# mLSTM stage: gate sums by store and broadcast load, queries and keys turned by 32x32 blocks and transfers

## What is computed

```python
proj = x @ w_in                                   # q, k, v, o, gates
k = k * 128 ** -0.5
log_i = gates[:4];  log_f = log_sigmoid(gates[4:])
# for each chunk of 128 tokens, each head, with the state (C, n, m):
b = cumsum(log_f)
d = b[:, None] - b[None, :] + log_i[None, :]      # causal, else -inf
m_t = max(b + m, max(d, -1))
w = exp(d - m_t)
qk = (q @ k.T) * w
num = qk @ v + s_inter * (q @ C)
den = sum(qk, -1) + s_inter * (q @ n)
h = num / max(abs(den), exp(-m_t))
# the state C, n from keys scaled by exp(g - m_new), and the values
```

## Time and profile before

| | |
|---|---|
| median of 3 runs | 1367.62 us (1362.96 to 1368.35) |
| the profiled execution | 1362.45 us, span 1360.7 us |
| TensorE busy | 1342.6 us, 99% of the span |
| GpSimd busy | 1144.6 us, 84% |
| VectorE busy | 653.0 us, 48% |
| ScalarE busy | 651.9 us, 48% |
| DMA queue q1 (SP) | 249.91 MB, 58.2% of 16 engines |
| mean granted clock of TensorE | 0.998 |

### The profile page before, as it was taken

One profiled execution on the slowest core, in us unless ns is written; L12 is line 12 of the kernel. 1 busy time (PEld: TensorE's weight loads), 2 busy tenths in 40 slices (PEclk: granted clock), 3 DMA queues, 4 the chain that ended last, 5 costly groups with the idle time before them and its releaser, 6 DMA issues.

```text
span 1360.7 us, 19512 instructions
## 1 busy us (share of the span) xinstructions
PE 1342.6 (99%) x6659; PEld 1115.8 (82%) x6659; DVE 653.0 (48%) x1584; ACT 651.9 (48%) x745; POOL 1144.6 (84%) x913
## 2 busy tenths in 40 slices
PE   8999999999999999999999999999999999989997
PEld 6888888888888888888888778888888887778886
DVE  6233344654333356523333885333346447874224
ACT  6444454546444456444444676444446344434431
POOL 6999977849999969999998539999978989789982
PEclk9999999999999999999999999999999999999999
DMA  8666654536665555766558426666545799997640
GB/s 275 216 209 204 204 186 141 186 107 225 196 192 193 197 171 168 240 210 214 185 185 217 139 70 205 209 196 194 193 155 179 221 268 270 256 247 230 206 164 32
DMA packets 230608, 263.75 MB, mean 194 GB/s; under 512 B 75884, under 2 KB 166804, under 8 KB 230548
## 3 DMA queue, kind: packets, MB, share of 16 engines
q1 hardware_dynamic: 201876, 249.91, 58.2%
q10 hardware_dynamic: 28672, 13.05, 3.7%
HBM read 253.49 MB, written 9.44 MB: 193 GB/s over the span
## 4 chain that ended last, share of the span: by engine, by line
PE 90%; DVE 5%; DMA 2%; ACT 1%; issue 1%; ACTq 1%; SPq 0%; DVEq 0%
PE tb L2203 9%; PE gu L2203 9%; PE acc L2113 7%; PE acc L2114 7%; PE acc L2116 7%; PE acc L2150 6%; PE acc L2153 6%; PE acc L2158 6%; PE gu L2113 5%; PE gu L2114 5%; PE tb L2209 4%; PE gu L2209 4%; PE gu L2116 3%; PE gu L2121 2%; DMA hidden_T<-h_bounce 1%; PE tb L2116 1%
## 5 line engine op out<-in xcount | busy, mean ns | idle before, releaser
L664 POOL TENSOR_TENSOR w_lo<-w_raw,w_hi 128x512 fp32r<-128x512 f32 x896 | 1139.6, 1317 | 189.0 <-ACT w_hi L697 186.6
L697 ACT CAST w_hi<-w_raw 128x2048 fp32r<-128x2048 f32 x225 | 428.0, 1910 | 185.9 <-DMA w_raw<-in_w_in 46.6
L2203 PE MATMUL gu<-xT,w_hi 128*128 128x512 f32 x512 | 202.4, 395 | 0.0
L2203 PE MATMUL tb<-xT,w_hi 128*128 128x512 f32 x512 | 202.2, 395 | 0.0
L2113 PE MATMUL acc<-w_hi,xT 128*128 128x512 f32 x496 | 197.9, 399 | 0.0
L2114 PE MATMUL acc<-w_lo,xT 128*128 128x512 f32 x496 | 193.8, 391 | 0.0
L2116 PE MATMUL acc<-w_hi,xT 128*128 128x512 f32 x468 | 183.1, 391 | 0.0
L1419 DVE TENSOR_TENSOR arena<-gu,arena 128x256 f32<-128x256 f32 x64 | 27.2, 425 | 300.6 <-PE gu L2203 300.6
L2209 PE MATMUL tb<-xT,w_lo 128*128 128x256 f32 x512 | 140.3, 279 | 0.0
L2209 PE MATMUL gu<-xT,w_lo 128*128 128x256 f32 x512 | 139.8, 279 | 0.0
L2113 PE MATMUL gu<-w_hi,xT 128*128 128x512 f32 x312 | 123.4, 395 | 1.1 <-ACT xT L742 1.1
(11 more groups left out here) (364 smaller groups left out, 1974.4 us busy)
## 6 DMA issues: line engine op xcount, KB each, us to landing
w_raw<-in_w_ffn_in SPq DMA_DIRECT2D x176, 512.0 KB, 4.7
w_raw<-in_w_ffn_out SPq DMA_DIRECT2D x88, 512.0 KB, 4.2
w_raw<-in_w_in SPq DMA_DIRECT2D x80, 512.0 KB, 4.8
w_raw<-in_mlstm_w_in SPq DMA_DIRECT2D x24, 512.0 KB, 4.3
w_raw<-in_w_ple_gate SPq DMA_DIRECT2D x16, 512.0 KB, 4.3
w_raw<-in_w_kv SPq DMA_DIRECT2D x16, 512.0 KB, 4.3
w_raw<-in_mlstm_w_out SPq DMA_DIRECT2D x8, 512.0 KB, 4.4
w_raw<-in_diff_w_q SPq DMA_DIRECT2D x8, 512.0 KB, 5.0
```

The lines of the kernel that those rows point to most:

```text
L664: ins = pool.tensor_tensor(w_lo[:, slot.spl, cols], w_raw[:, slot.raw, cols], w_hi[:, slot.spl, cols].bitcast(F32), ALU.subtract)
L697: nc.scalar.copy(w_hi[:, slot.spl, :], w_raw[:, slot.raw, :]).then_inc(hi_ready, 1)
L2203: return mm(pair_of(j), w_hi[:, slot.spl, at:at + P], xT[:, 4 * half + k, :, :].rearrange("p a c -> p (a c)"), start=(half == 0 and k == 0 ...
```

## The change

It has two parts.

*Gate sums.* `diag` and `spread` are gone. VectorE's a (128 x 8 values) is stored by SP to a DRAM tensor `m_a_rows` of 8 rows of 128, 4 bytes at a time; when that store has landed, SP loads the 1024 values as one row to all 128 partitions (`m_a_bc`, 512 KB). Both chunks' maxima read that SBUF area.

*Queries and keys.* VectorE turns them by 32x32 blocks into `m_blocks`, SP stores the blocks in their places of a DRAM tensor `m_bounce` (four transfers for the queries, four for the keys), and loads each back with one transfer. `turn_qk` and `turned_qk` are gone.

```diff
+            def store_qk(i):
+                sp.wait_ge(m_qk_turned, 2 * i + 2)
+                pieces = m_bounce[i].rearrange("n (j b) (i a) -> b (n j) i a", j=4, i=4)
+                for q in range(4):
+                    sp.dma_start(pieces[:, :, q, :], m_blocks[i][32 * q:32 * q + 32].rearrange("b (n a) -> b n a", a=32)
+                                 ).then_inc(m_qk_stored, 16)
+            def load_qk(i):
+                sp.wait_ge(m_qk_stored, 64 * (i + 1))
+                sp.dma_start((m_qT, m_kT)[i].rearrange("p h (t a) -> p (h t) a", t=TILES),
+                             m_bounce[i].rearrange("n p a -> p n a")).then_inc((m_q_landed, m_k_landed)[i], 16)
+            def spread_gates():
+                sp.wait_ge(m_a_ready, 1)
+                sp.dma_start(m_a_rows.rearrange("n s -> s n"), m_a, allow_slow_non_contiguous=True).then_inc(m_a_stored, 16)
+                sp.wait_ge(m_a_stored, 16)
+                sp.dma_start(m_a_bc.rearrange("p t c -> p (t c)"),
+                             m_a_rows.rearrange("(o n) s -> o (n s)", o=1).broadcast_to([P, D])).then_inc(m_a_spread, 16)
+            def after_mi(i):
+                if i == 10:
+                    store_qk(0)
+                if i == 11:
+                    spread_gates()
+            def after_mo(i):
+                if i == 0:
+                    load_qk(0)
+                    store_qk(1)
+                if i == 1:
+                    load_qk(1)
...
+                dve.wait_ge(m_copied, 4)
+                for i, src in enumerate((m_qn, m_kn)):
+                    for t in range(TILES):
+                        to = m_blocks[i].rearrange("p (h t j a) -> p t h j a", h=MH, t=TILES, j=4)[:, t]
+                        v.transpose(to, src[:, t, :].rearrange("p (h j b) -> p h j b", h=MH, j=4)
+                                    ).then_inc(m_qk_turned, 1)
...
-                def diag(t):
-                    v.tensor_tensor(m_diag.rearrange("p (h c) -> p h c", h=MH),
-                                    ident[:].unsqueeze(1).broadcast_to([P, MH, P]),
-                                    m_a[:, 4 * t:4 * t + 4].unsqueeze(2).broadcast_to([P, MH, P]),
-                                    ALU.mult).then_inc(m_diag_ready, 1)
...
-                                    tb[:, 0, :].rearrange("p (h c) -> p h c", h=MH),
+                                         m_a_bc[:, t, :].rearrange("p (h c) -> p h c", h=MH),
...
-                diag(0)
                 take(2)
+                dve.wait_ge(m_a_ready, 1)
+                dve.wait_ge(m_a_spread, 16)
                 causal_max(0)
...
-                diag(1)
+                causal_max(1)
                 take(3)
 
                 dve.wait_ge(m_last_in_psum, 1)
                 link(v.tensor_copy(m_lrow, tb[:, 1, 24:32]))
-                causal_max(1)
...
-                def spread(t):
-                    pe.wait_ge(m_diag_ready, t + 1)
...
-                    mm(tb[:, 0, :], ones, m_diag, start=True, stop=True).then_inc(m_spread, 1)
...
-                chunk(3, {0: lambda: spread(0)})
+                chunk(3)
...
-                def turn_qk(i):
...
                 def scores(t):
-                    pe.wait_ge(m_pl_ready, 3 + t)
+                    pe.wait_ge(m_q_landed, 16)
+                    pe.wait_ge(m_k_landed, 16)
...
-                chunk(4, {0: lambda: turn_qk(0), 1: lambda: turn_qk(1), 2: scores_and_state,
+                chunk(4, {2: scores_and_state,
                           3: on_state_and_scores})
```

More of the change, by code:

```diff
@@ L239, in program @@
          m_hz, m_prev, m_n, m_qn_den) = (area(at + 16 + 8 * i, 8 if i < 16 else 4) for i in range(19))
-        m_diag = area(1280, 512)
+        m_a_bc = area(8192, TILES, 512)
+        m_blocks = [area(at, 1024) for at in (10240, 11264)]
+        m_a_rows = nc.dram_tensor("m_a_rows", (8, P), F32, kind="Internal").ap()
+        m_bounce = [nc.dram_tensor(f"m_bounce{i}", (8, P, P), F32, kind="Internal").ap() for i in range(2)]
         m_gT = arena[0:8, 1280:1536]
@@ L418, in program @@
         m_w_ready = sem("m_w_ready")
-        m_pl_in_psum = sem("m_pl_in_psum")
-        m_pl_ready = sem("m_pl_ready")
+        m_qk_turned = sem("m_qk_turned")
+        m_qk_stored = sem("m_qk_stored")
+        m_q_landed = sem("m_q_landed")
+        m_k_landed = sem("m_k_landed")
         m_ksc_ready = sem("m_ksc_ready")
@@ L610, in _ @@
             ffn("F0", A["w_ffn_in"][0, 0], A["w_ffn_out"][0, 0])
-            linear(S["MI"], A["mlstm_w_in"][0], [512 * c for c in range(6)])
-            linear(S["MO"], A["mlstm_w_out"][0], both)
+            linear(S["MI"], A["mlstm_w_in"][0], [512 * c for c in range(6)], after=after_mi)
+            linear(S["MO"], A["mlstm_w_out"][0], both, after=after_mo)
             ffn("F1", A["w_ffn_in"][0, 1], A["w_ffn_out"][0, 1])
@@ L951, in mlstm @@
                 ahead(At(s0 + 8))
[L953 to L960, removed]
                 act.wait_ge(m_exps, 1)
@@ L1586, in causal_max @@
+                def causal_max(t):
+                    link(v.tensor_tensor(m_am[:, t, :].rearrange("p (h c) -> p h c", h=MH),
+                                         m_a_bc[:, t, :].rearrange("p (h c) -> p h c", h=MH),
+                                         causal[:, 0:P].unsqueeze(1).broadcast_to([P, MH, P]), ALU.add))
                     link(v.tensor_reduce(m_mx[:, 4 * t:4 * t + 4],
                                          m_am[:, t, :].rearrange("p (h c) -> p h c", h=MH), AX, ALU.max))
-                diag(0)
@@ L2383, in mlstm @@
                 chunk(2, {0: turn_gates, 3: cumulate})
-                def spread(t):
-                    pe.wait_ge(m_diag_ready, t + 1)
-                    if t:
-                        pe.wait_ge(m_am_ready, t)
-                    mm(tb[:, 0, :], ones, m_diag, start=True, stop=True).then_inc(m_spread, 1)
-                chunk(3, {0: lambda: spread(0)})
+                chunk(3)
                 pe.wait_ge(m_last_rhs, 1)
                 mm(tb[:, 1, 24:32], last_row, m_last, start=True, stop=True).then_inc(m_last_in_psum, 1)
-                spread(1)
                 pe.wait_ge(m_last_in_psum, 1)
-                def turn_qk(i):
[L2400 to L2403, removed]
-                        for h in range(MH):
-                            ins = nc.tensor.transpose(tb[:, w % 2, tok(h)], (m_qn, m_kn)[i][:, w % 2, tok(h)],
-                                                      ident[:])
-                        ins.then_inc(m_pl_in_psum, 1)
                 def scores(t):
-                    pe.wait_ge(m_pl_ready, 3 + t)
+                    pe.wait_ge(m_q_landed, 16)
+                    pe.wait_ge(m_k_landed, 16)
                     for h in range(MH):
```

17 lines of the change are left out of this document (5 added, 12 removed).

## The result

| | before | changed |
|---|---|---|
| median of six runs each, same chip | 1364.68 us (1362.52 to 1368.35) | 1373.34 us (1371.33 to 1377.89) |
| ratio, 95% interval | | 1.0069 (1.0050 to 1.0088) |
| span of the profiled execution | 1360.7 us | 1376.1 us |
| TensorE busy, instructions | 1342.6 us, 6659 | 1343.6 us, 6639 |

The account below looks back on a forecast made before the run. TensorE's instructions bound the kernel; 3.73 us leave it, but a 5.0 us wait and 1.6 us of clock start the state matmuls 2.9 us later. Mean 1365.3 plus 2.9 gives 1368.2, named 1369; range 1361 to 1377.

Parts of the forecast that it names:

- The forecast proper: Whole run: state matmuls start 2.9 us later; a loss of 1 to 5.5 us, chance 0.5.
- the slow store: Rival at the gate sums' store: 4-byte pieces need 10.5 us, loss 7.9, 1373.2 us from the mean; chance 0.2.
- the prediction's own signs: Profile checks: TensorE waits about 5 us at L2394's successor, store lands near 5.5 us, keys land before the scores.
- TensorE comes to L2418: L2394's successor: TensorE, without its first spread, arrives at 246.5, then stands 5.0 us.
- store issued: Sync queue: gate sums ready at 236.4, store issued at 237.4 behind the last slot of input weights.
- store to broadcast's issue: Gate sums' store: lands 5.5 us after issue, at 242.9, behind 1 MB of weights complete at 241.41.
- broadcast to the first maximum: Load of one 4 KB row to 128 partitions: takes 4.4 us, landing at 247.3.
- to L2418: VectorE from first maximum to L2394's right-hand side: 4.2 us with GpSimd contention, 3.7 today; ready at 251.5.
- L2418 to state matmuls: TensorE: 0.12 for L2394, 9.15 to the state matmuls and 1.6 for the clock, starting at 262.4.
- The clock: TensorE behind its 5 us wait: half clock makes eight 512-column matmuls 0.2 us longer each, 1.6 us.
- The keys: Sync queue: four key stores issued at 1.05 us each, keys loaded by 258.4, before the scores at 261.5.
- The block turns: VectorE: four 32x32 block turns at 1.08 us, 4.3 in all, hidden in a 5.87 us hole before the cumulated sums.

Follow-up runs that it names:

- e3: The change, with VectorE turning the gate sums by 32x32 blocks so they are stored in 128-byte pieces, same queue place; 1366.34 us, ratio 1.0025.
- e9: The change, with gate sums stored token by token as 128 pieces of 32 bytes, the maximum reading with a stride; 1372.01 us, ratio 1.0068.
- e5: The change, with the 4-byte gate-sum store issued by ScalarE on its own queue; 1373.73 us, ratio 1.0086.
- e1: Gate half of the change alone: gate sums through DRAM, queries and keys turned on TensorE as before; 1374.37 us, ratio 1.0090 to before.
- e10: e9, with the key stores issued while the gate sums' store is under way; 1370.5 us, ratio 1.0044.
- e12: The change, with gate sums turned and stored in 128-byte pieces on SP, key stores early, L2418 behind chunk 4's first piece; 1368.24 us, ratio 1.0032.
- e8: e3, with gate sums stored and loaded on ScalarE's queue, key stores early, L2418 behind chunk 4's first piece; 1369.02 us, ratio 1.0059.
- e6: The change, with L2418 moved behind the second piece of chunk 4; 1374.92 us, ratio 1.0092.
- e4: The change, with nine extra 512-column fp32 matmuls, results unread, ahead of L2418; 1375.6 us, ratio 1.0113.
- e2: Query and key half of the change alone: block turns and transfers, gate sums on TensorE as before; 1367.34 us, ratio 1.0018 to before.

## Why the prediction was right, and where it was off

Direction, place and mechanism held: 1373.34 lies in the range, and the wait stands at L2394's successor, ended by VectorE, which had waited for the broadcast. The size was off threefold. The forecast proper, a loss of 1 to 5.5 us with a chance of 0.5, did not come; the measured 8.7 lies in the range because the range took in the slow store. Two of the prediction's own signs were not met: the store's landing is far from 5.5 us, and the keys did not land before the scores. Counted from the copy of the cumulated sums (the first row is no term of the sum):

| step | predicted | measured in the changed kernel |
|---|---|---|
| TensorE comes to L2418 | 11.0 | 11.0 (257.19 - 9.32 - 236.90) |
| store issued | 1.9 | 1.8 |
| store to broadcast's issue | 5.5 | 10.35 |
| broadcast to the first maximum | 4.4 | 6.2 |
| to L2418 | 4.2 | 1.95 |
| L2418 to state matmuls | 10.9 | 12.2 |
| **stage** | **26.9** | **32.5** |

The prediction reads today's stage by the chain of the earlier trace rows, 24.0 us, where the timeline has 23.84.

**The store** is the term that was mis-sized, by 4.85 us of the 5.6 by which the stage is longer than forecast. The prediction said: "The nearest row is a store of 1024 pieces of 128 bytes: eight were issued in 8.37 us, 1.05 each", and held the landing to be the end of the weights ahead plus that. The weights did end in time (242.7); the store landed 6.4 us behind them, with the DMA engines idle for most of it. For the larger pieces the rule of the sum, the end of the weights and about 1 us, held: 1.1 us in e3 and 0.7 in e9, where the weights were in at 241.5. Only the 4-byte form breaks it, and e5 shows that another queue does not help. The rival "a slow element store" is what happened: it had 10.5 us and +7.9, 1373.2, and got a chance of 0.2. That the median comes within 0.2 us of its 1373.2 is luck: the broadcast, VectorE and the clock were off as well and nearly cancel. The page's rule named there (the Trainium skill, DMA: Bandwidth & Descriptors, Specifications: below 512 B a read-modify-write) does not tell the cases apart: the 32- and 128-byte pieces lie below 512 B as well and landed in 4.3 us. So the size of 10 us has no explanation here.

**The broadcast** took 6.1 us, outside the 3.6 to 5.8 of the earlier trace rows and 1.7 above the value chosen. The traffic issued behind it does not explain this. In e3 and e9 the same weights, query load and key stores follow it, and it took 4.4 and 4.5 us; in e1 only weights follow it, and it took 5.9. What differs is the start. In the changed kernel nothing moves for 2 us after its issue at 249.06; in e3, issued at 243.57, the data flow within 1 us (a window of each, columns as above, then the next one of e3):

```profile
249.00:251.00 2.00, 0.00 (x0) 0.00 (x0) 0.00 (x0) 0.00 (x0) 2.00 (x2) 0.94 0.00 0
...
243.50:244.50 1.00, 1.00 (x6) 0.84 (x5) 0.00 (x0) 1.00 (x1) 1.00 (x2) 1.00 0.00 0
244.50:245.50 1.00, 1.00 (x6) 0.81 (x5) 0.00 (x0) 0.98 (x2) 1.00 (x2) 1.00 0.89 262
```

All five kernels with the 4-byte store have a broadcast of 5.9 to 6.1 us. Whether that store or the idle engines before the broadcast delay its start was not separated. The broadcast took 5.5 to 5.7 us in e10 to e12, beside key stores, and 7.7 in e8.

**VectorE** was 2.25 us quicker than forecast. The maximum took 0.69, not 1.2, and no small operation up to L1626 was stretched, because GpSimd had stopped: ScalarE's next rounding is queued behind the maxima, so the late sums starved it. GpSimd in the changed kernel:

```profile
232.69 19.90 POOL L706 TENSOR_TENSOR w_lo<-w_raw,w_hi 128x512 fp32r<-128x512 f32 x16 [3.66 <-ACT w_hi L739]
260.04 2.54 POOL L706 TENSOR_TENSOR w_lo<-w_raw,w_hi 128x512 fp32r<-128x512 f32 x2 [7.44 <-ACT w_hi L739]
```

Where the sums come while GpSimd works, and the maximum reads without a stride, it took 1.24 in e8, 1.33 in e12 and 1.41 in e3, near the forecast's 1.2. A longer delay took its contention away. The two rows behind that 1.2 do not separate the cases, though: GpSimd worked beside both executions of L1573, the one of 1.73 and the one of 0.68.

**The clock** fell as forecast, to 0.50 in the window shown. L2418 to the scores took 11.23 us less 0.64 of waiting, 10.6, against 0.12 + 9.15 - 0.89 = 8.4 by the earlier trace rows: 2.2 us where 1.6 were counted. The granted clock was 0.50, 1.2 GHz, until about 261.0, that is for 3.8 us, which account for most of it: half of them, 1.9 us, as an estimate. A shorter wait did not make this cheaper. Behind the 4.1 us of e3 the clock stayed at 0.50 for 6.7 us, and L2418's successor to the state matmuls took 12.7 us, more than the 12.2 of the change. So e3's wait is 5.3 us shorter, but its stage only 4.8.

**The keys** came 0.64 us too late instead of 3 us early. Two things hid in that margin: their stores started about 6 us later than planned, behind the slow store, and took 7.90 us to issue (four at 1.05 were counted; the query stores, in a quiet stretch, took 2.84). e6 shows how near this limit lies: take the first wait away and it holds the stage.

**The block turns** are hidden as forecast, and cheaper: four in 2.49 us, 0.62 each, not 1.08; VectorE still stood 3.48 us before the cumulated sums.

**The resolution** was better than assumed. The prediction said that 0.5% cannot be told from no change; the interval of the ratio, 1.0050 to 1.0088, is about 0.2% to either side and lies clear of 1.

## What to carry to other kernels

A round trip through DRAM is priced by the landing of its store, in the form in which it is written: issued directly behind 1 MB of weights, 4 KB in 4-byte pieces took 10 us or more, in 32- or 128-byte pieces 4.3. So look for a row with that piece size, and if there is none, give the slow end a large chance. Count the whole way to the consumer: TensorE came to its wait 11.0 us after the cumulated sums (13.7 with L2418 behind the first piece of chunk 4), and the shortest way through DRAM and VectorE took 15.0 (e3; 16.3 in e12). Count what the clock costs behind the wait as well: 3.4 to 6.7 us at half speed in these kernels. When a wait is removed by filling or moving work and nothing is gained, read which wait grew: here the key stores stood on SP's queue behind the late landing, and were late with it.

## What the runs showed beyond that

- The 4-byte store landed in 10.0 to 10.8 us in all five kernels that have it, and the changed one's profile shows 0 GB/s for 6 us of them. In all five there are 1 MB of weights ahead of it or beside it. Whether the 4 bytes or the 1024 pieces do it was not separated: e9 changes both. The prediction's row of 1024 pieces of 128 bytes, at 1.05 us of issue each, speaks for the size of the piece, without proof.
- The clock fell behind a wait of 2.1 us as well (e4), and only about 2 us after work had resumed: 0.94, then 0.50. Behind the 1.48 us of e2 and the second wait of e4, 1.71 us, it stayed at 1.00. So a wait of 2 us need not be free, and some shorter ones were.
- A VectorE operation with two SBUF inputs, one of them strided, took 5.81, 4.02 and 1.66 us beside GpSimd's subtractions against 1.08 alone; two of them ended 0.85 us after GpSimd's run. Unstrided ones were held in some executions too: 14.27 us (0.55 us after GpSimd's run), 4.15 and 5.34 us. The Trainium skill (SBUF — State Buffer, Who interferes with whom) describes an exclusive lock on a port pair that VectorE shares with GpSimd. It fits that all of these ran beside GpSimd, but one of GpSimd's subtractions takes 1.25 us, so the long ones were held over several of them. Why some are held so long and others, at the same place, are not, stays open.
